# Hybrid encoder layer: the last three down tiles in token halves, down weights prepared in a pipeline, the mixer's first tiles and evictions in another order

## What is computed

```python
h = layer_norm(concat([meta, x]), ln_in_g, ln_in_b)              # 16 + 512 tokens, width 1024
h = layer_norm(DN_ALPHA*h + 0.5*swiglu(h, gate1, up1, down1))     # D_FF = 2816
h = layer_norm(DN_ALPHA*h + token_mixer(h, w_in, ..., w_out))     # windowed attention || gated linear attention
h = layer_norm(DN_ALPHA*h + 0.5*swiglu(h, gate2, up2, down2))
return h[:, N_META:]
```

## Time and profile before

| what | value |
|---|---|
| three runs | 1083.59, 1091.71, 1092.06 us (median 1091.71) |
| the profiled execution | 1082.67 us, its span 1080.9 |
| TensorE, VectorE, ScalarE busy | 997.0, 720.4, 382.2 us |
| first FFN's down tiles end | 396.1 |
| projections of the mixer | 412.8 to 575.9 |
| output projection ends | 681.1 |
| second FFN's down tiles end | 1059.0 |

### The profile page before, as it was taken

How to read it: one execution, slowest core, us unless ns; L and a number is a source line. 1 busy time by engine, 2 the same in 40 slices (tenths; PEclk the granted TensorE clock), 3 DMA queues, 4 the chain that set the end, 5 groups by cost and what they waited for, 6 DMA issues and landing times.

```text
span 1080.9 us, 16392 instructions
## 1 busy us (share of the span) xinstructions
PE 997.0 (92%) x6605; PEld 654.4 (61%) x6605; DVE 720.4 (67%) x1186; ACT 382.2 (35%) x488; POOL 32.3 (3%) x96
## 2 busy tenths in 40 slices
PE   3999999999899988999996889699999999989995
PEld 2888888888688875985564434434444444434443
DVE  6766666668755667767659757666666667966645
ACT  5422222224411126754334741462222223531105
POOL 0000000000000000000000000000000000000000
PEclk9999999999899998999998999889999999999998
DMA  5323232323232121111211003112323223322202
GB/s 203 107 79 109 85 110 84 109 86 110 105 108 85 68 78 32 62 64 42 77 40 40 1 1 117 40 73 83 116 78 116 96 98 127 111 78 86 104 1 79
DMA packets 23808, 88.76 MB, mean 82 GB/s; under 512 B 2907, under 2 KB 3251, under 8 KB 23763
## 3 DMA queue, kind: packets, MB, share of 16 engines
q1 hardware_dynamic: 22752, 87.17, 22.7%
q10 hardware_dynamic: 1011, 0.99, 0.3%
HBM read 86.05 MB, written 2.10 MB: 82 GB/s over the span
## 4 chain that ended last, share of the span: by engine, by line
PE 75%; DVE 16%; ACT 6%; issue 2%; DMA 0%; ACTq 0%; POOL 0%; DVEq 0%
PE PS L553 35%; PE PS L593 20%; PE PS L648 8%; DVE cmax L1413 3%; DVE wsp L1435 3%; PE PS L944 3%; ACT wsp L1059 2%; PE PS L510 2%; PE PS L632 1%; DVE big L1513 1%; ACT H L1053 1%; PE PS L770 1%; DVE X L1363 1%; PE PS L922 1%; PE PS L766 1%
## 5 line engine op out<-in xcount | busy, mean ns | idle before, releaser
L553 PE MATMUL PS<-xs,wsp 128*128 128x264 f16 (+1 forms) x3168 | 472.7, 312 | 7.5 <-ACT xs L1051 4.0
L553 PEld LDWEIGHTS PS<-xs,wsp 128*128 128x128 f16 x3168 | 311.0, 98 | 168.4 <-issue 9.6
L1059 ACT ACTIVATE wsp<-stage,wscale 128x2048 f16<-128x2048 f32 (+2 forms) x73 | 156.5, 2144 | 369.9 <-DVE wscale L1399 198.0
L1435 DVE SCALAR_TENSOR_TENSOR wsp<-stage,wscale,wsp 128x2048 f16<-128x2048 f32 (+2 forms) x73 | 184.6, 2529 | 114.3 <-ACT wsp L1059 114.3
L593 PE MATMUL PS<-big,wsp 128*128 128x264 f16 (+1 forms) x1584 | 238.6, 314 | 11.6 <-DVE big L1513 9.5
L593 PEld LDWEIGHTS PS<-big,wsp 128*128 128x128 f16 x1584 | 155.8, 99 | 94.1 <-DVE big L1513 12.8
L1413 DVE TENSOR_REDUCE cmax<-stage 128x1 f32<-128x2048 f32 (+2 forms) x73 | 179.7, 2462 | 3.9
L1447 DVE SCALAR_TENSOR_TENSOR big<-PS,oscale,tmp_a 128x528 f32 (+3 forms) x44 | 33.4, 759 | 75.7 <-ACT tmp_a L1066 75.6
L1066 ACT ACTIVATE tmp_a<-PS,oscale 128x528 f32<-128x528 f32 (+1 forms) x44 | 30.5, 694 | 136.1 <-PE PS L553 136.1
L648 PE MATMUL PS<-xs,wsp 128*128 128x264 f16 (+1 forms) x384 | 67.0, 328 | 0.1
L2007 POOL PARTITION_ALL_REDUCE call<-cmax x73 | 27.9, 382 | 979.1 <-DVE cmax L1413 979.1
(11 more groups left out here) (208 smaller groups left out, 685.1 us busy)
## 6 DMA issues: line engine op xcount, KB each, us to landing
stage<-in_gate SPq DMA_DIRECT2D x44, 512.0 KB, 3.4
stage<-in_up SPq DMA_DIRECT2D x44, 512.0 KB, 4.2
stage<-in_down SPq DMA_DIRECT2D x32, 704.0 KB, 4.9
stage<-in_w_in SPq DMA_DIRECT2D x16, 512.0 KB, 4.4
stage<-in_w_out SPq DMA_DIRECT2D x8, 512.0 KB, 4.4
X<-in_x SPq DMA_DIRECT2D x4, 512.0 KB, 6.2
out_T<-H SPq DMA_DIRECT2D x8, 256.0 KB, 2.0
stage<-in_w_in SPq DMA_DIRECT2D x2, 576.0 KB, 4.4
```

Source lines behind the costliest of these rows:

```text
L553: return nc.tensor.matmul(dst, w, x, start=k == 0 and wp + xp == 0, stop=k == KD - 1 and xp == 1)
L1059: nc.scalar.activation(wsp[:, slot, 0, 0:cols], stage[:, slot, 0:cols], ACT.Copy, scale=wscale[:, slot:slot + 1]).then_inc(w_hi, 1)
L1435: nc.vector.scalar_tensor_tensor(wsp[:, slot, 1, 0:cols], stage[:, slot, 0:cols], wscale[:, one], wsp[:, slot, 0, 0:cols], ALU.mult, ALU.s ...
```

## The change

Down stage: tiles 5, 6 and 7 are done in two token halves, in the order 0 1 2 3 4, (5 6 7 of half 0), (5 6 7 of half 1). Their weights have places of their own (`w_extra`, in the arena), and chunks are loaded and prepared in the order 0, 1, 5, 2, 3, 6, 4, 7. The layer norm of half 0 is done between the tiles of half 1. Mixer: `first_proj_tiles` and the next two tiles are done by halves, gq0 is done around `gates(0)` and gq1 before `gates(1)`; ScalarE evicts and ScalarE and VectorE prepare weights in a changed order there. Layer norm 2: the low part of the next weights is written ahead of the last residual, their maximum behind the centring, their scale behind the reciprocals. A small Sqrt is done ahead of each layer norm. The last store is done in 16 pieces instead of 8.

```diff
+N_FULL = 5
+DN_ORDER = [0, 1, 5, 2, 3, 6, 4, 7]
...
@@ SP
-                with sp.Fori(0, N_DN // 2) as i:
-                    for t in range(2):
-                        sp.wait_ge(w_ready, DN[f] - 1 + t + 2 * i)
-                        load_halves(down[f][2 * i + t], (DN[f] + t) % 2, DN_COLS)
+                for n, q in enumerate(DN_ORDER):
+                    sp.wait_ge(w_ready, DN[f] + n - 1)
+                    load_halves(down[f][q], (DN[f] + n) % 2, DN_COLS)
...
+            for h in range(2):
+                for k in range(KD):
+                    sp.wait_ge(h_ready, ln_late(3, KD * h + k) + 1)
+                    sp.dma_start(out[k][:, h * SEQ // 2:(h + 1) * SEQ // 2], H[:, k, token_half(3, h)]).then_inc(out_done, 16)
@@ PE
+                for q in range(N_FULL):
+                    down_tile(f, q)
+                down_tile(f, 5, 0)
+                down_tile(f, 6, 0)
+                down_tile(f, 7, 0, (KF - 3, lambda: sum_tiles(L, 0)))
+                down_tile(f, 5, 1, (8, lambda: mean(L, 0)))
+                square_sums(L, 0)
+                down_tile(f, 6, 1)
+                down_tile(f, 7, 1, (KF - 3, lambda: sum_tiles(L, 1)))
...
             def mixer_projections():
-                first_proj_tiles()
-                proj_tile(GK + 1)
+                first_proj_tiles(0)
+                square_sums(1, 1)
+                early_proj_tile(GK + 1, 0)
+                early_proj_tile(GQ, 0)
+                first_proj_tiles(1)
+                early_proj_tile(GK + 1, 1)
                 gates(0)
+                early_proj_tile(GQ, 1)
+                proj_tile(GQ + 1)
                 gates(1)
-                for n in range(GQ, GV + NCH + 1):
+                for n in range(GV, GV + NCH + 1):
                     proj_tile(n)
@@ ACT
             def layer_norm(L, chunk=None):
+                nc.scalar.activation(warm[:, L + 1:L + 2], eps[:, 1:2], ACT.Sqrt).then_inc(warmed, 1)
...
+                for n in range(2, N_DN):
+                    q = DN_ORDER[n]
+                    c = DN[f] + n
+                    if q < N_FULL:
+                        act.wait_ge(res_ready_b, N_RES * f + q - 1)
+                    act.wait_ge(w_scale, 4 * c + 3)
+                    nc.scalar.activation(w_down(f, q, 0), stage[:, c % 2, 0:DN_COLS], ACT.Copy,
+                                         scale=wscale[:, c % 2:c % 2 + 1]).then_inc(w_hi, 1)
...
+                for h in range(2):
+                    layer_norm_half(2 * f + 1, h)
...
                 proj_out(GK + 1)
+                proj_out(GQ)
                 gates_abs(0)
+                projection_hi(2)
+                proj_out(GQ + 1)
                 gates_abs(1)
-                projection_hi(2)
-                gates_ln(0)
-                proj_out(GQ)
-                proj_out(GQ + 1)
+                gates_ln(0, GV)
                 projection_hi(3)
-                proj_out(GV)
                 decays(0, 0)
                 proj_out(GV + 1)
@@ DVE
             def layer_norm(L, chunk):
                 for h in range(2):
                     centre(L, h)
-                if chunk is not None:
-                    chunk_scale(*chunk)
+                c = GU[1] + 1
+                chunk_max(c, c % 2, c // 2, KD * 2 * P)
...
+                chunk_scale(*chunk)
                 dve.wait_ge(rstd_ready, 2 * L)
...
+                next_max(2)
+                next_scale(2)
+                next_max(3)
+                next_lo(2)
+                next_scale(3)
+                down_residual(f, 0)
+                next_lo(3)
+                next_max(4)
+                next_scale(4)
+                next_max(5)
+                next_scale(5)
+                down_residual(f, 1)
+                next_lo(4)
+                next_lo(5)
+                next_max(6)
+                next_scale(6)
+                down_residual(f, 2)
+                next_max(7)
+                next_lo(6)
+                next_scale(7)
+                next_lo(7)
+                down_residual(f, 3)
+                next_max(8)
+                next_scale(8)
+                next_max(9)
+                down_residual(f, 4)
+                next_lo(8)
+                next_scale(9)
+                down_residual(f, 5, 0)
+                next_lo(9)
+                down_residual(f, 6, 0)
+                down_residual(f, 7, 0)
+                centre(L, 0)
+                down_residual(f, 5, 1)
+                half_rstd(L, 0)
+                half_norm(L, 0, 0, 4)
+                down_residual(f, 6, 1)
+                half_norm(L, 0, 4, KD)
+                down_residual(f, 7, 1)
+                centre(L, 1)
+                half_rstd(L, 1)
+                half_norm(L, 1, 0, KD)
...
             def mixer_projections():
-                projection_lo(1)
                 sink_columns()
                 projection_max(2)
+                projection_scale(2)
                 gate_floor(0)
+                projection_lo(2)
                 gate_floor(1)
-                projection_scale(2)
-                projection_lo(2)
                 projection_max(3)
+                projection_scale(3)
                 gates(0)
-                projection_scale(3)
                 gates(1)
...
                 for t in range(2):
+                    if last and t:
+                        chunk_lo(c + 1, (c + 1) % 2, cols)
+                    residual_tile(2 * n + t, t, c % 2)
-            chunk_lo(GU[1], GU[1] % 2, GU_COLS)
-            chunk_max(GU[1] + 1, (GU[1] + 1) % 2, (GU[1] + 1) // 2, GU_COLS)
```

More of the change, by code:

```diff
@@ L86 @@
 KF_A = KF - 3
+N_FULL = 5
+DN_ORDER = [0, 1, 5, 2, 3, 6, 4, 7]
+DN_AT = [DN_ORDER.index(q) for q in range(N_DN)]
+N_RES = 2 * N_DN - N_FULL
+RES = {1: 0, 2: N_RES, 3: N_RES + KD}
+LN_DONE = {1: 0, 2: 2 * KD, 3: 3 * KD}
+X_DONE = {0: 0, 1: KD, 2: 3 * KD}
 HID, HID_B, MIX = [0, 3], [1, 4], 2
@@ L493, in _, with sum_tiles @@
+            sp.wait_ge(out_done, 2 * 16 * KD)
         @block.tensor
         def _(pe):
[L495 to L499, removed]
+            def sum_tiles(L, h):
+                pe.wait_ge(x_summed, sums_before(L) + (N_SUM if L == 2 or h == 0 else KD))
+                nc.tensor.matmul(PS[:, ln_bank(L, 0, h), 0:ln_width(L)], ones[:, :], x_sum[:, token_half(L, h)], start=True, stop=False)
@@ new lines, in mean, with square_sums @@
+            def mean(L, h):
+                if L == 2:
+                    pe.wait_ge(*((res_half, 1) if h == 0 else (res_done, 2 + RES[3])))
+                else:
+                    pe.wait_ge(res_done, 2 + RES[L] + N_DN + (N_DN - N_FULL) * h)
+                nc.tensor.matmul(PS[:, ln_bank(L, 0, h), 0:ln_width(L)], ones[:, :], X[:, KD - 1, token_half(L, h)],
+                                 start=False, stop=True).then_inc(mean_ready, 1)
+            def square_sums(L, h):
+                for k in range(KD):
+                    n = ln_step(L, h, k)
+                    pe.wait_ge(squared, n + 1)
+                    nc.tensor.matmul(PS[:, ln_bank(L, 1, h), 0:ln_width(L)], ones[:, :], squares[:, n % 4, 0:ln_width(L)],
+                                     start=k == 0, stop=k == KD - 1).then_inc(sq_added, 1)
@@ L501, in layer_norm @@
             def layer_norm(L):
                 for h in range(2):
[L503 to L505 removed]
+                    mean(L, h)
                 for h in range(2):
[L507 to L511 removed]
+                    square_sums(L, h)
@@ L572, in gu_tile, with down_tile @@
                 mm.then_inc(gu_ready, 1)
-            def res_tile(late, r, s, w, src, kt, k_sem=None, k0=0, norm=None, split_at=None, before_b=None):
+            def down_tile(f, q, h=None, between=None):
+                i = q if h != 1 else q + N_DN - N_FULL
+                s = i % 2
+                r = RES[2 * f + 1] + i
+                pe.wait_ge(w_ready, DN[f] + DN_AT[q] + 1)
                 pe.wait_ge(res_done, r + 1)
-                for k in range(kt):
-                    if norm is not None and k == kt - 3:
-                        sum_tiles(norm)
-                    if k == split_at:
+                for k in range(KF):
+                    if between is not None and k == between[0]:
+                        between[1]()
+                    if k == KF_A:
@@ L597, in ffn @@
+                mm.then_inc(res_ready_b, 1)
             def ffn(f):
@@ L976, in _ @@
             ffn(1)
-            layer_norm(3)
+            mean(3, 1)
+            square_sums(3, 1)
         @block.scalar
@@ L1158, in gates_ln @@
                 nc.scalar.activation(ln, ln, ACT.Exp, scale=-1.0).then_inc(gate_exp, 1)
+                if between is not None:
+                    proj_out(between)
                 act.wait_ge(gate_exp, j + 1)
@@ new lines, in ffn @@
+                for n in range(2):
+                    down_scales(n)
+                next_max(2)
[13 more added lines that the diff above has]
+                next_max(6)
```

258 lines of the change are left out of this document (159 added, 99 removed).

## The result

The changed kernel takes 1096.08 us in the middle of 14 runs (1092.47 to 1099.17); the kernel before, timed beside it, took 1091.16 (1082.78 to 1092.26). The ratio over all these runs is **1.0079, 95% interval 1.0057 to 1.0101**: slower by 0.8%; the two medians alone would give 1.0045, since the runs of the kernel before spread over 9 us. The forecast was 1086 us and no difference; 1096.08 is 1.1 above the end of its range. Timed again later (1097.81 us), the same kernel gave 1.0087 (1.0056 to 1.0118).

A forecast was written before the change was run, and what follows sets the result against it. TensorE, busy 92% of the span, was taken as the bound. Mixer's start 0, second layer norm -5.4 and second FFN +4.0 gave about -1.5 us, put on the middle 1087.65: 1086 us, range 1068.3 to 1095.

The forecast's parts named there:

- Part 1: Down stages of both FFNs: added TensorE work, and tiles waiting for weights 3.8 us in the first, 6.9 in the second.
- part 2: First layer norm and mixer's start: -2.3 + 2.2 us, about 0, with the first FFN's 3.8 us of waits inside.
- Together 3.8 us: First FFN's down stage: tile 3 0.4 us late and tile 4 3.4 late for VectorE's low parts.
- 6.9 us: Second FFN's down stage: weights of slots 3, 4 and 6 late by 1.9, 0.95 and 4.0 us.
- slot 6's load: First FFN: load of the seventh chunk prepared (slots count from 0), for tile 4; VectorE waits 2.6 us for it.
- rival C: Waits of 3.4 and 4.0 us before tile 4 lower the granted clock: +4.5 us, 1085.7 on the profiled scale; chance 0.17.
- One k per 0.8 us: Second half of the first layer norm: its x parts come at this pace and reach 422.7 us.
- The stand in front of GV+3: Mixer: TensorE stands 7.7 us before tile GV+3 until ScalarE evicts GV+1; GV+3 starts 2.3 us earlier, not 10.
- The moved sums and the halving: Down stages: square sums and mean moved in, 3.95 us in each FFN; halved tiles, +0.8 us in the second.
- Rival A: Weight preparation keeps up in both FFNs, 0 late: -3.8 and -6.9 us, 1070.5 on the profiled scale; chance 0.20.
- Rival B: Mixer: the stand before GV+3 doesn't appear: -7.7 - 2.2 us, 1071.3 on the profiled scale; chance 0.09.
- rival D: Down stages: slow landings of two loads per FFN, each us above 5.6 costing about 4 in all; up to 1097; chance 0.13.

The follow-up runs named there:

- the natural order: The changed kernel with down weights prepared in the order of use, 0 to 7, and VectorE's list ordered to suit: 1078.6 us, ratio 0.9899 to the kernel before.

## Why the prediction was wrong

**Where it failed.** The places and the causes of the losses were right; three terms were too small or left out, and the time went past the upper end of the range. Part 1 is short in two of them, part 2 in one. By cause, the 11.9 us that were missing are 3.7 of longer waits, 4.2 of clock behind tile 4 and 3.8 at the first projection; the rest cancels.

- *"Together 3.8 us" and "6.9 us"*: measured 7.1 and 7.3. In the first FFN tile 4 was 4.95 late and not 3.4. The step that failed is "slot 6's load, issued at 321.5, lands at 327.1": it was issued 0.8 us later and took 7.2 us instead of 5.6, so its maximum began at 329.57. What follows has the worked length (low part done 12.7 us behind that; worked 12.6). Tile 2, worked as level, was 1.66 late: the low part came 0.55 later than worked, and tile 1 ended 1.0 sooner, at a granted clock of 0.90 from 283.5 to 299.8 us where the earlier trace rows has 0.82.
- *The clock behind those waits* stood outside the sum, as rival C at 0.17. It was the case: 1.5 and 2.7 us in the trace, all of it gone when TensorE was kept busy. The prediction had priced the same mechanism behind the longer stand in the mixer (2.2; measured 2.7) and left it out of the sum behind stands worked as 3.4 and 4.0 us, although show it behind three stands of 4.5 to 4.7 us, and nothing in them says that a stand a little shorter is free.
- *"One k per 0.8 us" and "5.9 us" for the first half of the first projection*: measured 1.00 and 7.4. I took 112 ns for each matmul; the pairs of a 32-wide and a 128-wide load make it 149. I had no row of it, but the trace of the kernel before shows the same thing: 0.22 us in front of each change of width, and 0.78 us for six loads (419.8 to 428.2 us), 130 ns each. The pace of the rows was taken from "ScalarE's two activations of 0.38 per k": at half the tokens they start 0.50 us apart, where a full row's start 0.72 apart, so halving the row does not halve them. Together 3.8 us up to the second gate. (The 10.7 us that the prediction lists for the second half hold the 5.4 of early tiles in front of them; its 436.8 counts these once.)

**What was right.** The stand in front of GV+3 came, from the chain that was worked out (6.58 us for 7.7): the experiment with the evictions moved shows its cause. It is 1.1 shorter since the table load counted in the chain (1.28, at 452.76) was done while ScalarE waited for VectorE. The moved sums and the halving cost about what they were put at; the clock and one stand hide part of the difference, as told at the natural order. The second layer norm gave 5.7 for 5.4, the last one 6.9 for 7.7: its eight outputs of 256 columns took 0.50 us each and not 0.38, the same mis-sizing as in the first projection. Rival A (nothing late) didn't occur, but the natural order makes it true: its 1070.5 on the profiled scale stands against 1078.36 there, with the mixer's start still slow. Rival B is what the evictions' order gave, at under half its price (4.1 of 9.9 us). Of rival D one landing of four came: it was 1.6 over and its tile 1.55 later than worked. The range had left D's own 1097 outside, and the bounds of 6 and 9 us for the waits too; with either in it 1096.08 would have been inside.

**The sum.** To the forecast's -1.5 on the profiled scale come 7.5 up to the third gate, 3.9 in the second FFN, 0.8 at the end, less 0.3 in the layer norm: 11.9, so +10.4, and 4.7 of the attention's clock make the 15.1. The forecast's 1086 plus 11.9 is 1097.9, for 1096.08 measured. That this is near is partly luck: the forecast stood on 1087.65 for the kernel before, whose median was 1091.16 here and 1085.84 to 1087.31 each time it was timed later.

## What to carry to other kernels

When preparation runs ahead of its consumer, order it by when each piece is wanted, and look at what stands in front of the late piece on its engine: here a maximum for a tile 30 us away stood in front of the low part that TensorE was waiting for, and one line was worth 0.8%. Price a new wait on TensorE with the clock behind it, not with its length alone. And where a stand is removed, look for what comes next before counting its whole length: here the third gate came 7.6 us sooner and the attention 4.1, with 1.8 given to other stands and 1.7 to the clock. And half a row is not half the time: ScalarE's activations took 0.50 us for half the tokens and 0.72 for all.

## What the runs showed of the hardware

- Behind stands of 4.2 to 5.4 us a tile took 1.4 to 2.8 us longer in five profiles, behind 2.45 us 1.6 (16.64 for 15.02), behind 1.66 and less nothing. With most of the stand filled by 36 matmuls of no use nothing was lost. Stands do not explain every fall of the clock: the one at 510.65 had none over 0.62 us in the 30 us before it.
- Alternating weight loads of 32 and 128 columns cost 149 to 150 ns per 264-column matmul, loads of 128 alone 119; before, in runs of six loads of one width, it was 130.
- GpSimd's reduction over partitions takes 0.35 us, and 3.18 where VectorE's low part (two large inputs from SBUF) had started 0.18 us ahead of it; moved apart, 0.35 again. It ended 0.22 us behind the low part (342.48 and 342.26). The Trainium skill, "SBUF — State Buffer", SBUF: two separate sides, gives this as a lock on a shared port that one side holds for its whole instruction; the trace agrees. It cost almost nothing here, since the scale stood behind the low part anyway.
- One 1.44 MB load took 7.2 to 7.7 us in eight profiles, at the same place of the program, with or without another beside it, where the same slot's load in the second FFN took 5.9 to 6.3. An instruction packet of about 1 us lay in the slow one each time; that it is the cause wasn't tested.
- An unchanged stretch, the attention, took 100.4 to 108.3 us in thirteen profiles, with a granted clock (620 to 650 us) of 0.94 in the two shortest and 0.76 to 0.90 in the others. One profile against one profile could not have told a loss of 8 us from none.
